# Hymba layer, projection phase: a block's finishing placed inside its own dense products, feature tiles reordered, turns of x alternating with the first pair's products

## What is computed

```python
h = rms_norm(x, pre_mix_norm)                   # x: 2048 x 1024
proj = h @ w_in                                 # 2304 columns
u = proj[..., :1792]                            # r, k, v (512 each), decay lora 64, alpha lora 64, gate lora 128
u = u + mu_shift * (token_shift(u) - u)
r, k, v, wl, al, gl = split(u)
w_log = -softplus(-(w0 + tanh(wl) @ w_decay_up)) - 0.5
decay = exp(-exp(w_log))
alpha = sigmoid(a0 + al @ w_aaa_up)
g = sigmoid(gl) @ w_gate_up
kk = normalised per head (k * k_k)
k_mod = k * (1 + (alpha - 1) * k_a)
bonus = sum_head(r * k_mod * r_k) * v
pooled = (mean over the last 2, 4, 8, 16 tokens - proj[..., 1792:]), then @ w_pool per group of 128, * pool_scale
```

## Time and profile before

| | us |
|---|---|
| median of 3 runs | 2852.91 (2849.73 to 2869.15) |
| the profiled execution: time / span | 2858.78 / 2857.0 |
| PE busy, DVE busy, ACT busy, POOL busy (share of the span) | 88%, 55%, 42%, 15% |
| projection phase, span start to the first load of the next phase | 713.1 |
| recurrence and output projection, to about | 1375 |
| MLP, to the end | 2857.0 |

### The profile page before, as it was taken

How to read it: one execution, slowest core, us unless ns; L and a number is a source line. 1 busy time by engine, 2 the same in 40 slices (tenths; PEclk the granted TensorE clock), 3 DMA queues, 4 the chain that set the end, 5 groups by cost and what they waited for, 6 DMA issues and landing times.

```text
span 2857.0 us, 41434 instructions
## 1 busy us (share of the span) xinstructions
PE 2516.3 (88%) x16164; PEld 2048.5 (72%) x16164; DVE 1562.1 (55%) x1947; ACT 1192.4 (42%) x1842; POOL 438.5 (15%) x340
## 2 busy tenths in 40 slices
PE   6998887863388885996999999999999999999996
PEld 4776666642377774885788887888887888878885
DVE  0074626373566552543556566665666666566665
ACT  4446454433133333453444444344444334544432
POOL 2453424330222222442000000000000000000000
PEclk9999999986688787998999999999999999999998
DMA  5335334333544534576632344333444223443321
GB/s 142 98 111 169 112 114 129 110 116 128 127 112 121 145 96 126 185 220 194 217 99 88 103 147 141 95 103 102 125 152 121 88 88 111 139 133 90 101 73 74
DMA packets 488645, 353.34 MB, mean 124 GB/s; under 512 B 73101, under 2 KB 439101, under 8 KB 487997
## 3 DMA queue, kind: packets, MB, share of 16 engines
q1 hardware_dynamic: 408060, 282.22, 33.1%
q10 hardware_dynamic: 80448, 69.22, 7.6%
HBM read 271.69 MB, written 79.69 MB: 123 GB/s over the span
## 4 chain that ended last, share of the span: by engine, by line
PE 48%; DVE 3%; ACT 1%; DMA 1%; issue 0%; SPq 0%; ACTq 0%; DVEq 0%
PE p_bank L123 16%; PE p_bank L124 16%; PE p_bank L125 16%; DVE p_acc L1995 1%; DVE p_x L1998 1%; ACT p_dump L1908 1%; DMA p_hT_lo<-scratch_h_lo 1%; DVE p_up_lo L1939 0%; DVE p_dn_lo L1944 0%; DVE p_cv L1964 0%; DVE p_cv L1959 0%; DVE p_cv L1954 0%; DVE p_acc L1984 0%; ACT p_a_hi L1891 0%; SPq L1810 0%
## 5 line engine op out<-in xcount | busy, mean ns | idle before, releaser
L123 PE MATMUL p_bank<-p_hT_hi,p_up_hi 128*128 128x512 f32 x1408 | 549.2, 390 | 25.6 <-DMA p_hT_lo<-scratch_h_lo 25.6
L124 PE MATMUL p_bank<-p_hT_lo,p_up_hi 128*128 128x512 f32 x1408 | 549.0, 390 | 0.0
L125 PE MATMUL p_bank<-p_hT_hi,p_up_lo 128*128 128x512 f32 x1408 | 548.9, 390 | 0.0
L1984 DVE TENSOR_TENSOR p_acc<-p_bank,p_acc 128x512 f32<-128x512 f32 x320 | 221.2, 691 | 199.1 <-PE p_bank L125 191.5
L123 PEld LDWEIGHTS p_bank<-p_hT_hi,p_up_hi 128*128 128x128 f32 x1408 | 264.8, 188 | 82.2 <-issue 25.8
L124 PEld LDWEIGHTS p_bank<-p_hT_lo,p_up_hi 128*128 128x128 f32 x1408 | 264.8, 188 | 55.6
L125 PEld LDWEIGHTS p_bank<-p_hT_hi,p_up_lo 128*128 128x128 f32 x1408 | 264.8, 188 | 55.4
L123 PE MATMUL p_bank<-p_dn_hi,p_a_hi 128*128 128x512 f32 x704 | 281.6, 400 | 15.1 <-DVE p_acc L1981 9.7
L124 PE MATMUL p_bank<-p_dn_lo,p_a_hi 128*128 128x512 f32 x704 | 281.0, 399 | 0.0
L125 PE MATMUL p_bank<-p_dn_hi,p_a_lo 128*128 128x512 f32 x704 | 280.8, 399 | 0.0
L1954 DVE SCALAR_TENSOR_TENSOR p_cv<-p_ub,p_cpar,p_cv 128x512 f32<-128x512 f32 x176 | 127.5, 746 | 251.0 <-ACT p_cv L1880 251.0
(11 more groups left out here) (189 smaller groups left out, 3929.6 us busy)
## 6 DMA issues: line engine op xcount, KB each, us to landing
p_up_raw<-in_w_up SPq DMA_DIRECT2D x176, 512.0 KB, 5.0
p_dn_raw<-in_w_down SPq DMA_DIRECT2D x88, 512.0 KB, 4.3
p_w_raw<-in_w_in SPq DMA_DIRECT2D x72, 512.0 KB, 3.9
p_xin<-in_x SPq DMA_DIRECT2D x8, 1024.0 KB, 6.1
p_m_raw<-scratch_mix SPq DMA_DIRECT2D x16, 512.0 KB, 4.1
p_x<-in_x SPq DMA_DIRECT2D x16, 512.0 KB, 4.4
scratch_x<-p_x ACTq DMA_DIRECT2D x16, 512.0 KB, 2.8
scratch_h_hi<-p_h_hi ACTq DMA_DIRECT2D x16, 512.0 KB, 5.5
```

The lines of the kernel that those rows point to most:

```text
L123: nc.tensor.matmul(out, lhs_hi, rhs_hi, start=start, stop=False)
L124: nc.tensor.matmul(out, lhs_hi, rhs_lo, start=False, stop=False)
L125: return nc.tensor.matmul(out, lhs_lo, rhs_hi, start=False, stop=stop)
L1984: nc.vector.tensor_tensor(dst, bank[:, 4 + n % 4, :], dst, ALU.add).then_inc(s_acc, 1)
```

## The change

1. Finishing moves from the next block's dense products into its own. Tiles are reordered (lora, gate, k, r, v, pool, the pool groups from the widest window down) so that what the finishing needs first is computed first. The fifth iteration disappears. Pooling's widest group runs at the end of the block on DVE, the other three after the next block's `hT_lo`; the pool products (`small(b, 0)`) therefore stand behind the next block's first pair. The second gram half and the turn of `dec` stand in the next block's first pair as well, the first gram half behind the last pair.
2. The turn of step k alternates with the dense steps k-2 of tiles 0 and 1 together; before, all turns came first.
3. `low_w(f+2)` comes ahead of `diff(f)` on GpSimd, one of each per tile; before, up to three diffs of the block before followed each `low_w`.
4. `store_ab` is 4 stores of 128 KB on SP's queue in place of 16 of 32 KB on ACT's; the layout of that scratch tensor changes, and the next phase's view with it.
5. At the start, x and the weights are loaded alternately, `gain` and `ident` have a semaphore of their own, and `high_w(0)`, `high_w(1)` stand among the norm's steps. The turns no longer wait for all parameters.
6. Semaphores are split by purpose (a single store counter became five). `cinv` is no longer overwritten: for blocks after the first one multiply-and-subtract takes the place of two short steps.

The order behind each piece that the diff below leaves out:

- PE: `small` after pair 1 and 2 decay and alpha; 3 gate; 4 head sums, into `ptr`; 5 spread of the norms; 6 bonus sums; 7 turn of v; 8 `gram(b, 0)`. `small(b, 0)` waits for all four poolings of b-1 and for `a_rows`. A turn of step k waits for `hT_lo` of step k-2.
- ACT: after `read_proj(b, f)` and `high_w(f+2)` of tile f: f=2 tanh; 3 and 5 `decays_alphas`; 4 gate sigmoid; 7 `kk_squares`; 8 `gates`; 9 `kk_root`, `exp_inverse`; 10 `exps`; 12 to 14 norm of block b+1 (squares, root, scale); 15 `v_rows`, stores of bonus and bt; 16 store of at; 17 stores of rt and kt.
- DVE: `hT_lo`, poolings 1 to 3 of b-1, shifts 0 to 3, scans 0 and 1, shift 4, scans 2 and 3, dec, shift 5, k factor, k_mod, shifts 6 and 7, norm maximum, shift 8, reciprocal, shift 9, kk times the spread norms, bonus terms, shift 10, alpha by kk, alpha by einv, shifts 11 and 12, a, shift 13, bonus, reciprocal for b+1, r, k, pooling 0 (after the store of bonus has landed, since it works in `tmp`).

The core of the diff (removed bodies are those printed above):

```diff
-LORA, GATE, R0, K0, V0, POOL0 = 0, 1, 2, 6, 10, 14
+LORA, GATE, K0, R0, V0, POOL0 = 0, 1, 2, 6, 10, 14
 # SP
+                for b in range(BLOCKS):
+                    for f in range(FT):
+                        if b * FT + f >= 2:
+                            load_w(b * FT + f)
+                        if f == 3 and b + 1 < BLOCKS:
+                            sp.wait_ge(s_tr, ONE + (b + 1) * KT)
+                            load_x(b + 1, 0)
+                            load_x(b + 1, 1)
+                        if f == 4 and b > 0:
+                            store_ab(b - 1)
+                store_ab(BLOCKS - 1)
 # GpSimd
+                for b in range(BLOCKS):
+                    for f in range(FT):
+                        if b * FT + f + 2 < BLOCKS * FT:
+                            low_w(b * FT + f + 2)
+                        if f < SHIFTED:
+                            diff(b, f)
 # ACT, block b
+                    for k in range(KT):
...
+                        act.wait_ge(s_tr, ONE + b * KT + k + 1)
+                        nc.scalar.activation(hT_hi[:, k, :], ptr[:, k % 2, :], ACT.Copy, scale=gain[:, k:k + 1]).then_inc(s_hh, 1)
+                        if b > 0 and k == 0:
+                            read_ab(b - 1, 0)
+                        if b > 0 and k == 3:
+                            read_ab(b - 1, 1)
+                        if b > 0 and k == 6:
+                            a_rows(b - 1)
+                    for f in range(FT):
+                        n = b * FT + f
+                        read_proj(b, f)
+                        if n + 2 < BLOCKS * FT:
+                            high_w(n + 2)
+                        if f == 1 and b > 0:
+                            pool_out(b - 1)
...
 # DVE, block b
+                    low_hT(b)
+                    if b > 0:
+                        for x in range(1, PAIRS):
+                            pool(b - 1, x)
...
+                    for f in range(4):
+                        shift(b, f)
...
+                    if x == 0:
+                        dve.wait_ge(s_bst, ONE + b * 16 + 16)
 # PE
+                def small(b, pair):
+
+                    if pair == 0 and b > 0:
+                        pool_products(b - 1)
...
+                LAG = 2
+                for b in range(BLOCKS):
+
+                    for k in range(KT + LAG):
+                        if k < KT:
+                            turn_x(b, k)
+                        if b > 0 and k == 2:
+                            gram(b - 1, 1)
+                        if b > 0 and k == 5:
+                            a_turn(b - 1)
+                        if k >= LAG:
+                            pe.wait_ge(s_ht, ONE + b * KT + k - LAG + 1)
+                            for f in range(2):
+                                dense(b, f, k - LAG)
+                    small(b, 0)
+                    for pair in range(1, FT // 2):
                         for f in (2 * pair, 2 * pair + 1):
                             for k in range(KT):
+                                dense(b, f, k)
+                        small(b, pair)
+                gram(BLOCKS - 1, 1)
                 a_turn(BLOCKS - 1)
+                pool_products(BLOCKS - 1)
```

More of the change, by code:

```diff
@@ L258, in _, with load_x, load_w @@
             def _(sp):
[L259 to L265, removed]
+                def load_x(i, half):
+                    t = half * (TT // 2)
+                    sp.dma_start(xin[:, t:t + TT // 2, :], xv[:, bass.ds(i * TT + t, TT // 2), :]).then_inc(s_x[half], 16)
+                def load_w(n):
+                    f = n % FT
+                    if n >= 2:
                         sp.wait_ge(s_wh, ONE + n - 1)
@@ L329, in diff @@
                                             proj[:, f, HALO:HALO + TB], ALU.subtract).then_inc(s_diff, 1)
[L331 to L348, removed]
+                low_w(0)
+                low_w(1)
+                for b in range(BLOCKS):
[4 more added lines that the diff above has]
+                            diff(b, f)
             @block.scalar
@@ L432, in kk_squares, with kk_root, exp_inverse @@
                     act.wait_ge(s_kkr, ONE + b + 1)
+                    act.wait_ge(s_bst, ONE + b * 16)
+                    act.wait_ge(s_poolin, ONE + b * PAIRS)
                     nc.scalar.activation(tmp[:, :, :], kk[:, :, :], ACT.Square).then_inc(s_sqk, 1)
-                def finish_rows(b):
-                    read_ab(b, 0)
-                    a_rows(b)
-                    read_ab(b, 1)
-                    store_ab(b)
-                def exps(b):
+                def kk_root(b):
+                    act.wait_ge(s_nmax, ONE + b + 1)
+                    nc.scalar.activation(norm[:, :], norm[:, :], ACT.Sqrt).then_inc(s_nrt, 1)
+                def exp_inverse(b):
                     act.wait_ge(s_cum, ONE + b + 1)
@@ L550, in body @@
-                        if finish and pair == 7:
+                        if f == 9:
+                            kk_root(b)
+                            exp_inverse(b)
+                        if f == 10:
+                            exps(b)
+                        if f == 12 and more:
+                            for t in range(TT):
+                                norm_squares(b + 1, t)
+                        if f == 13 and more:
+                            norm_root(b + 1)
+                        if f == 14 and more:
+                            norm_scale(b + 1)
@@ new lines, in _ @@
+                        if f == 15:
+                            v_rows(b)
+                            act.wait_ge(s_bo, ONE + b + 1)
+                            store("bonus", tmp[:, :, :], b, s_bst)
+                            act.wait_ge(s_bt, ONE + b + 1)
+                            store("bt", alpha[:, :, :], b, s_btst)
+                        if f == 16:
+                            act.wait_ge(s_at, ONE + b + 1)
+                            store("at", dec[:, :, :], b, s_atst)
+                        if f == 17:
@@ L563, in _ @@
-                iterations(nc.scalar, body)
-                finish_rows(BLOCKS - 1)
+                            store("kt", um[:, K0:K0 + PAIRS, :], b, s_kst)
+                read_ab(BLOCKS - 1, 0)
+                read_ab(BLOCKS - 1, 1)
+                a_rows(BLOCKS - 1)
+                pool_out(BLOCKS - 1)
             @block.vector
             def _(dve):
-                K = 31
+                POOL_STEPS = sum(g + 1 for g in range(PAIRS))
                 def norm_reciprocal(i):
@@ L683, in _, with products @@
+                for x in range(1, PAIRS):
+                    pool(BLOCKS - 1, x)
             @block.tensor
             def _(pe):
-                pe.wait_ge(s_const, ONE + 1)
-                pe.wait_ge(s_par, ONE + 16 * NPAR)
-                def products(lhs, rhs):
+                def products(lhs, rhs, done):
                     for j in range(PAIRS):
                         last = nc.tensor.matmul(pm[:, j, :], lhs(j), rhs(j), start=True, stop=True)
-                    last.then_inc(s_mm, 1)
+                    last.then_inc(done, 1)
@@ L694, in rows, with decay_alpha @@
+                def decay_alpha(b, r):
+                    for j in range(2):
+                        for h in range(2):
+                            row = slice(64 * h, 64 * h + 64)
+                            last = nc.tensor.matmul(pm[:, 2 * h + j, :], wlora[row, (2 * r + j) * P:(2 * r + j + 1) * P], um[row, LORA, :],
+                                                    start=True, stop=True)
+                    last.then_inc(s_da, 1)
                 def rows(src, done):
@@ new lines, in turn_x @@
+                def turn_x(b, k):
+                    if b == 0 and k < 2:
+                        pe.wait_ge(s_xs, ONE + TT)
+                        pe.wait_ge(s_first, ONE + 32)
+                    elif k < 2:
+                        pe.wait_ge(s_xs, ONE + b * TT + TT)
+                        pe.wait_ge(s_nmax, ONE + b)
+                    else:
+                        pe.wait_ge(s_ht, ONE + b * KT + k - 1)
+                    for t in range(TT):
+                        last = nc.tensor.transpose(ptr[:, k % 2, t * P:(t + 1) * P], xin[:, t, k * P:(k + 1) * P], ident[:, :])
+                    last.then_inc(s_tr, 1)
@@ new lines, in dense @@
+                def dense(b, f, k):
+                    n = b * FT + f
+                    if k == 0:
+                        pe.wait_ge(s_wh, ONE + n + 1)
+                        pe.wait_ge(s_wl, ONE + n + 1)
+                        if n >= 2:
+                            pe.wait_ge(s_prf, ONE + n - 1)
+                    last = split_matmul(nc, ppr[f % 2][:, :], w_hi[f % 2][:, k, :], w_lo[f % 2][:, k, :],
+                                        hT_hi[:, k, :], hT_lo[:, k, :], k == 0, k == KT - 1)
+                    if k == KT - 1:
+                        last.then_inc(s_pr, 1)
```

597 lines of the change are left out of this document (278 added, 319 removed).

## The result

The changed kernel took 2776.19 us (median of 4, 2763.38 to 2780.1) against 2853.77 before (median of 4): ratio 0.9715 as recorded (the two medians alone give 0.9728), 95% interval 0.9672 to 0.9758. Forecast was 2782.

What follows compares the result with a forecast made beforehand. TensorE was taken to bound dense work, a four-engine chain of small steps the last 117.3 us. The end's 83.8 us and 9.3 in blocks 1 to 3, less 22 in block 0, gave 71.1 gained: 2782 us, range 2744 to 2812.

Steps and rivals of the forecast that it cites:

- The end of the phase: Chain behind the last dense matmul: 33.5 us in place of 117.3, bounds 29 to 38, a gain of 83.8.
- Block 1's start: Block 1 begins at 157 us in place of 135.3, since block 0 now carries its own finishing: 22 us lost.
- The wait that the change adds: TensorE waits 11.5 us before the pool products for DVE's poolings, bounds 5.3 and 14; 3.0 us of clock besides.
- P: Block period, work plus waits and clock losses: 151.1 us; the gain in terms of it is 524.4 - 3P.
- no collision: Rival: poolings avoid GpSimd's steps and the second half is on time; P = 140.5, time 2750; chance 0.22.
- The second half of a block: DVE and GpSimd collisions make `low_w(17)` 0.6 us late; with clock 3 us a block, bounds 0 to 10.
- DVE's chain is the bound: Rival for the second half: wide DVE passes meet `low_w`, TensorE waits before pairs 7 and 8; time 2812; chance 0.18.
- slower: Rival: a ring of waits over ACT, DVE and TensorE closes; loses from P = 175, 2884 us at P = 185; chance 0.04.
- The block's start: First pair: 2.9 us of waiting and 1.5 of clock; late pooling 0 delays the first `hT_lo` by 2 us.
- The alternation doesn't alternate: Rival: first pair takes 32 us against 23.9, 8 us a block; P = 159, time 2806; chance 0.10.

Runs made afterwards that it cites:

- e7: Changed kernel with the four gram stores issued by ACT, not SyncE, in blocks 1 to 3; 2779.04 us, ratio 0.9709 to the kernel before.
- c0: The changed kernel run again without any edit; 2778.36 us, ratio 0.9730 to the kernel before.
- e2: Changed kernel with the store of bonus issued earlier on ACT, ahead of `norm_scale`; 2764.53 us, ratio 0.9672 to the kernel before.
- e3: Changed kernel with the low weights of tiles 2 and 3 written by DVE behind the poolings, not GpSimd, in blocks 1 to 3; 2761.07 us, ratio 0.9661.
- e4: Changed kernel with the alternation undone: all turns first, then tiles 0 and 1 one after the other; 2762.99 us, ratio 0.9679 to the kernel before.
- e8: Changed kernel with the edits of e1 and e4 together; 2740.16 us, ratio 0.9599 to the kernel before.
- e1: Changed kernel with pool products and their readout moved from behind the first pair to half-way through tile 3; 2756.85 us, ratio 0.9659 to the kernel before.
- e6: Changed kernel with the edits of e1 and e2, and tile 1 three steps behind tile 0; 2731.72 us, ratio 0.9569 to the kernel before.

## Why the prediction was right

Its account in parts, forecast against profile, in us of the profiled execution:

- The end of the phase: 117.3 to 33.5 forecast, 30.4 measured. This is the gain: 86.9, of which the start and the blocks give 6.5 back. The chain ran as written. The turn of `dec` took 1.97, not 3.6, and the last store landed 4.0 us after its issue, not 5.9 (in the kernel before, the bonus store of the last block landed after 4.3; the 10.3 taken was the median of four). That part 1 of the change makes the gain is read from these stretches; no run undoes it, nor parts 3 and 6, and e7 tries part 4 for the queue alone.
- Block 1's start: 157 forecast, 153.17 measured (155.0 in c0). Blocks 1 to 3 to the last dense matmul: 451.2 forecast, 449.1 measured (151.2 and 150.2 from start to start of blocks 1 and 2, for 151.1). With the end's 3 us less than forecast, this is why the first load came at 632.8 and not near 642.
- The wait that the change adds: 11.5 forecast, 11.06 to 11.34 measured, with DVE's poolings of 12.7 for 13.3. Both ends of it came later than put, the pair's at 28.4 and not 22.4 (25.9 with the clock and the late `hT_lo` that P adds apart), the poolings' at 39.4 and not 33.9; both hang on the same late `hT_lo`, so their difference held (e2, where that one comes sooner, has both sooner and the wait at 11.06 still). e3 shows that GpSimd's weight steps make 4 us of it, so *no collision* is out (though taking them out gave 3.5 us a block, where the sum has 4.8 for them). The clock behind it cost 2.1 (5.71 for the products' 3.59), not 3.0.
- The second half of a block: 3 us late was forecast, nothing is. *DVE's chain is the bound* is out as well, and *slower* with it.
- The block's start: the first turns' wait was put at 2.9 and the late pooling 0 at 2; together 6.7 to 7.0 before the third turn, and the first pair ended 28.4 after the block's start, not 25.9. The mechanism was named; the size was off. I took the store's landing 7.5 us behind its issue at 7 us before the block's end, that is at 0.5; it was issued at 296.50, 7.8 before the turns, and landed near 305.5, 9 us later, at 1.2. The larger part is pooling 0: it took 5.8 us (305.57 to 311.35), not 4.0, since its first sum met a weight step of GpSimd and took 2.78. I had looked for that collision only in poolings 1 to 3. The two errors inside P, 3 too much and 2.5 too little, cancelled; that P came out within 1 us is in part luck.
- *The alternation doesn't alternate* was wrong as put (turns and L123 alternate from 28.07 on, 1.8 us a step). But the forecast gave the alternation as a gain. In e4 and e8 undoing it takes 7 and 10 us off the blocks; in blocks 2 and 3 of e4 it is worth nothing either way: I had priced `low_w(2)` behind a pair whose two tiles end together only for block 0, and the pool products' wait hid it in the rest.

Two sums of the prediction are slightly off: the terms of the end add up to 33.1, not 33.5, and the parts of a block to 127.6, where P uses 127.2. Together they would move the forecast by less than 1 us.

The median's gain, 77.6, and the phase's, 80.3, agree within what runs of one kernel differ by.

## What to carry to other kernels

A chain of small steps that runs uncovered at the end of a pipeline is worth most of its length when it is moved under the work it belongs to (here 86.9 of 117.3 us); what the move costs is read from the one wait in each round whose input is made last. Two tiles that end together leave no cover for the steps that prepare the third: let the first end sooner. A buffer that a store still reads is a wait for a DMA landing; issue that store first.

## What the runs showed that I had not expected

The same idle stretch does not always cost the same behind it. At fourteen places in eight of the profiles TensorE waits 3.65 to 3.69 us for `low_w(2)` ahead of tile 2. The 36 matmuls behind it took 9.8 to 9.9 us at four of them, 10.7 to 11.1 at nine and 8.3 at one (e1, block 3); behind the 1.65 of e6 they took 8.3 in all four blocks. So a saved wait of that kind gives back up to 2.9 us more than its length, and how much is not known beforehand.

The end stretch, the same code in all kernels, goes by its granted clock too (0.84 and 0.67 here). e4, then e1:

```profile
597.05:625.84 28.79, 10.99 (x89) 7.97 (x88) 8.09 (x16) 10.01 (x18) 0.00 (x0) 0.84 0.58 199
```

```profile
579.50:612.49 32.99, 15.19 (x88) 10.37 (x88) 8.08 (x16) 10.01 (x18) 0.00 (x0) 0.67 0.51 174
```

TensorE is busy for 4.2 us more in the second, and the stretch is 4.2 longer.

The untouched phases behind took between 2136.8 and 2151.9 us in the profiles above, most of it in the recurrence, whose short matmuls are run at a clock that differs from one execution to the next. The recurrence of e6, then of e3, the same code:

```profile
587.00:1002.50 415.50, 310.87 (x6464) 274.84 (x6464) 223.66 (x477) 133.31 (x289) 100.36 (x168) 0.79 0.41 110
```

```profile
625.30:1026.20 400.90, 295.98 (x6464) 260.82 (x6464) 223.08 (x477) 133.31 (x289) 100.75 (x168) 0.83 0.43 114
```

DVE, ACT and GpSimd are busy for the same time in both; TensorE differs by 14.9 us and the stretch by 14.6. What sets the clock there was not tried. It is why edits of a few us are judged here by the phase that they touch.
